# Token tiles and first weights issued from two queues, and the first two projected tiles made in halves

## What is computed

```
h    = rmsnorm(x, norm1_g)                      # x: 512 x 1024
proj = h @ w_in                                 # w_in: 1024 x 3080
fq, fk, fv, f_logit, sq, sk, sv = split(proj)
fox  = forgetting_attention(fq, fk, fv, cumsum(log_sigmoid(f_logit + b_f)))
sb   = stick_breaking_attention(sq, sk, sv)
x    = x + concat(rmsnorm(fox), rmsnorm(sb)) @ w_out
x    = x + moe(rmsnorm(x), ...)                 # 32 experts, top 4
y    = rmsnorm(x)
```

## Time and profile before

| | |
|---|---|
| median of 3 executions | 1460.68 us |
| lowest and highest | 1460.29 and 1463.81 us |
| the profiled execution, its own time | 1463.33 us |
| its span in the trace | 1461.6 us |
| busy share of the span | PE 98%, DVE 90%, ACT 75%, POOL 26% |
| DMA moved | 451.31 MB |

### The profile page before, as it was taken

How to read it: one execution, slowest core, us unless ns; L and a number is a source line. 1 busy time by engine, 2 the same in 40 slices (tenths; PEclk the granted TensorE clock), 3 DMA queues, 4 the chain that set the end, 5 groups by cost and what they waited for, 6 DMA issues and landing times.

```text
span 1461.6 us, 22338 instructions
## 1 busy us (share of the span) xinstructions
PE 1431.5 (98%) x7068; PEld 1164.4 (80%) x7068; DVE 1308.5 (90%) x1520; ACT 1100.6 (75%) x1345; POOL 380.2 (26%) x177
## 2 busy tenths in 40 slices
PE   9999999999999999999999999999999999999995
PEld 7777787787888888888888888888888888888884
DVE  5778765579999999999999999999999999999997
ACT  5668554357888887888888888888888888888884
POOL 3000000050433333333333333333333333333222
PEclk9999999999999999999999999999999999999998
DMA  8021022269999999999999999999999999999953
GB/s 260 14 74 58 29 87 77 107 240 396 410 391 394 397 389 389 385 382 374 373 380 386 367 379 381 374 371 387 377 368 380 377 377 376 378 376 380 365 219 126
DMA packets 98058, 451.31 MB, mean 309 GB/s; under 512 B 11427, under 2 KB 23715, under 8 KB 65250
## 3 DMA queue, kind: packets, MB, share of 16 engines
q1 hardware_dynamic: 90706, 434.16, 77.1%
q0 software_dynamic: 7312, 16.63, 5.0%
HBM read 440.46 MB, written 18.48 MB: 314 GB/s over the span
## 4 chain that ended last, share of the span: by engine, by line
PE 87%; DVE 7%; ACT 3%; DMA 2%; issue 1%; POOL 0%; SPq 0%; ACTq 0%; POOLq 0%; DVEq 0%
PE zpair L2201 47%; PE bank L2201 24%; PE bank L1901 2%; PE bank L1789 2%; PE bank L1791 2%; PE bank L1790 2%; PE bank L2151 1%; PE bank L2159 1%; DVE stage_lo L1212 1%; DVE lbuf L1292 1%; PE zpair L2170 1%; DMA x_scratch<-qk,sidx 1%; DVE pt_lo L1301 1%; DVE lbuf L1288 0%; DVE cols L1309 0%
## 5 line engine op out<-in xcount | busy, mean ns | idle before, releaser
L1212 DVE TENSOR_TENSOR stage_lo<-ring,stage_hi 128x1024 fp32r<-128x1024 f32 x796 | 947.1, 1220 | 41.0 <-ACT stage_hi L788 12.5
L788 ACT CAST stage_hi<-ring 128x1024 fp32r<-128x1024 f32 x796 | 828.0, 1054 | 171.4 <-PE zpair L2201 141.6
L2201 PE MATMUL zpair<-stage_hi,act_hi 128*128 128x512 f32 x1024 | 322.6, 396 | 0.3 <-DVE act_lo L1605 0.3
L668 POOL COPY sidx<-gtab 96x1 int32 (+1 forms) x31 | 230.3, 7428 | 350.3 <-ACT qk L1098 350.3
L2201 PE MATMUL zpair<-stage_hi,act_lo 128*128 128x512 f32 x1024 | 316.6, 390 | 0.0
L2201 PE MATMUL zpair<-stage_lo,act_hi 128*128 128x512 f32 x1024 | 316.2, 390 | 0.3 <-DVE stage_lo L1212 0.2
L2201 PEld LDWEIGHTS zpair<-stage_lo,act_hi 128*128 128x128 f32 x1024 | 192.1, 188 | 42.3 <-DVE stage_lo L1212 1.1
L2201 PEld LDWEIGHTS zpair<-stage_hi,act_lo 128*128 128x128 f32 x1024 | 192.2, 188 | 41.1
L2201 PEld LDWEIGHTS zpair<-stage_hi,act_hi 128*128 128x128 f32 x1024 | 187.4, 188 | 43.8 <-issue 7.9
L2201 PE MATMUL bank<-stage_hi,act_hi 128*128 128x512 f32 x510 | 159.8, 395 | 0.0
L2201 PE MATMUL bank<-stage_lo,act_hi 128*128 128x512 f32 x510 | 157.1, 389 | 0.0
(11 more groups left out here) (301 smaller groups left out, 1424.8 us busy)
## 6 DMA issues: line engine op xcount, KB each, us to landing
ring<-in_w SPq DMA_DIRECT2D x384, 1024.0 KB, 8.1
ring<-in_w_in SPq DMA_DIRECT2D x12, 1024.0 KB, 5.3
ring<-in_w_out SPq DMA_DIRECT2D x4, 1024.0 KB, 4.8
xs_all<-in_x SPq DMA_DIRECT2D x4, 512.0 KB, 5.7
ring<-in_x SPq DMA_DIRECT2D x4, 512.0 KB, 3.7
tn_scratch<-qk SPq DMA_DIRECT2D x4, 512.0 KB, 2.8
x_scratch<-ring SPq DMA_DIRECT2D x4, 512.0 KB, 3.6
ring<-x_scratch SPq DMA_DIRECT2D x4, 512.0 KB, 5.8
```

Source lines behind the costliest of these rows:

```text
L668: nc.gpsimd.tensor_copy(sidx[:], gtab[:, i:i + 1] if isinstance(i, int) else gtab[:, bass.ds(i, 1)]).then_inc(sidx_copied, 1)
L788: nc.scalar.copy(dst, src).then_inc(split_hi, 1)
L1212: nc.vector.tensor_tensor(dst, src, hi_ap.bitcast(F32), ALU.subtract).then_inc(split_lo, 1)
L2201: mm = pe.matmul(bank[b0 + h][:], w[:, k, :], m[:, j % STAGES, h * BANK:(h + 1) * BANK], start=start and w is T_hi and m is stage_hi, stop ...
```

## The change

SP now issues `g1row` first, then `x` tiles 0 and 2, W0 and W2, and from W4 on as before. ACT issues `x` tiles 1 and 3, W1 and W3, ahead of its table load. On ACT and DVE, the casts and rests of the first four halves are followed by the weight pieces 0 and 1, and only then comes token tile 3. On PE, projected tiles 0 and 1 are both made in halves of 256 tokens: tile 0 on the first half of the tokens, then the transposes of token tile 3, tile 1 on the first half, tile 0 and tile 1 on the second. Tile 1 gets bank 1 in place of bank 5. Ten fillers are added on PE before the first projection.

```diff
         def proj_bank(tile):
 
-            return bank[4 + (tile + (tile >= F_AT)) % 2] if tile else bank[0]
+            return bank[4 + (tile + (tile >= F_AT)) % 2] if tile > 1 else bank[tile]
...
         def _(sp):
-            for t in range(TT):
+            sp.dma_start(g1row[0:1, :], norm1_g[0:1, :]).then_inc(g1_in, 16)
+            for t in (0, 2):
                 sp.dma_start(xs[t], x_d[t * P:(t + 1) * P, :]).then_inc(x_in[t], 16)
-                if t == 0:
-                    sp.dma_start(g1row[0:1, :], norm1_g[0:1, :]).then_inc(g1_in, 16)
-
-            for n in range(W_IN_LOADS):
-                kind, r = n // 6, n % 3
-                c0 = (0 if kind else 3 * HW + NH) + r * HW + n // 3 % 2 * 2 * P
+            for n in (0, 2, *range(4, W_IN_LOADS)):
                 if n >= 4:
                     old = n - 4
                     sp.wait_ge(split_lo, 3 * (2 * (old // 3) + 1) + old % 3 + 1)
...
+                sp.dma_start(w_in_slot(n), w_in_columns(n)).then_inc(full[w_slot(n)], 16)
...
+            for t in (1, 3):
+                act.dma_start(xs[t], x_d[t * P:(t + 1) * P, :]).then_inc(x_in[t], 16)
+            for n in (1, 3):
+                act.dma_start(w_in_slot(n), w_in_columns(n)).then_inc(full[w_slot(n)], 16)
             nc.scalar.preload_act_table_set("natural_log_exp_and_others")
...
             h_scale(2)
-            h_cast(0)
-            h_cast(1)
+            for j in range(4):
+                h_cast(j)
+            hi_early(0)
+            hi_early(1)
             h_scale(3)
-            h_cast(2)
-            h_cast(3)
-            hi_early(0)
             for j in range(4, 8):
                 h_cast(j)
...
             h_scaled(2)
-            h_rest(0)
-            h_rest(1)
+            for j in range(4):
+                h_rest(j)
+            lo_early(0)
+            lo_early(1)
             h_scaled(3)
-            h_rest(2)
-            h_rest(3)
-            lo_early(0)
             for j in range(4, 8):
                 h_rest(j)
...
+            for j in range(6):
+                if j in (2, 4):
+                    pe.wait_ge(consts, 4)
+                    keep_busy(4, 4 if j == 2 else 8)
+                turn_h(j)
+            pe.wait_ge(h_lo, 1)
+            keep_busy(0, 10)
             pe.wait_ge(h_lo, 4)
             keep_busy(1, 8)
...
+            def project_half(tile, half):
+
+                pe.wait_ge(split_lo, tile + 1)
+                pe.wait_ge(h_lo, 4 * half + 4)
+                ts = slice(2 * half * P, 2 * (half + 1) * P)
...
-            pe.wait_ge(split_lo, 1)
-            for half in range(2):
-                pe.wait_ge(h_lo, 4 * half + 4)
-                for k in range(KT):
-                    project_half(k, half)
-            for tile in range(1, 3):
-                for k in range(KT):
-                    project(tile, k)
+            project_half(0, 0)
+            turn_h(6)
+            turn_h(7)
+            project_half(1, 0)
+            project_half(0, 1)
+            project_half(1, 1)
+            for k in range(KT):
+                project(2, k)
```

More of the change, by code:

```diff
@@ L399, in turned_at, with w_in_slot, w_in_columns @@
             return obank[m] if s % TT else zpair[s % 2][:, m, :]
+        def w_in_slot(n):
+            return slot(w_slot(n)).rearrange("p (k n) -> p k n", k=KT)
+        def w_in_columns(n):
+            kind, r = n // 6, n % 3
+            c0 = (0 if kind else 3 * HW + NH) + r * HW + n // 3 % 2 * 2 * P
+            return w_in_d.rearrange("(k p) n -> p k n", p=P)[:, :, c0:c0 + 2 * P]
         def moe_slot(c):
@@ L460, in _ @@
                     sp.wait_ge(split_lo, 3 * (2 * (old // 3) + 1) + old % 3 + 1)
-                sp.dma_start(slot(w_slot(n)).rearrange("p (k n) -> p k n", k=KT),
-                             w_in_d.rearrange("(k p) n -> p k n", p=P)[:, :, c0:c0 + 2 * P]).then_inc(full[w_slot(n)], 16)
+                sp.dma_start(w_in_slot(n), w_in_columns(n)).then_inc(full[w_slot(n)], 16)
             for m in range(W_OUT_LOADS):
@@ L941, in scale_of_norm @@
                 nc.scalar.activation(rm[:, cs], rsm[:, cs], ACT.Exp, scale=-0.5).then_inc(rsm_ready, 1)
-            hi_early(1)
             hi_early(2)
@@ L1362, in add_oproj @@
                                                op0=ALU.mult, op1=ALU.add).then_inc(x2_add, 1)
-            for g in range(1, STAGES):
+            for g in range(2, STAGES):
                 lo_early(g)
@@ L1811, in _, with turn_h @@
             pe.wait_ge(consts, 1)
-            for j in range(2 * TT):
+            def turn_h(j):
                 t, h = j // 2, j % 2
-                if j in (2, 4):
-                    pe.wait_ge(consts, 4)
-                    keep_busy(4, 4 if j == 2 else 8)
                 pe.wait_ge(h_norm, t + 1)
@@ L1820, in _ @@
                 mm.then_inc(h_turned, 1)
+            for j in range(6):
[5 more added lines that the diff above has]
+            keep_busy(0, 10)
             pe.wait_ge(h_lo, 4)
             keep_busy(1, 8)
[L1824 to L1829, removed]
+            def project_half(tile, half):
[3 more added lines that the diff above has]
+                for k in range(KT):
+                    ks = slice(k * P, (k + 1) * P)
+                    mm = three(proj_bank(tile)[:, ts], stage_hi[:, tile, ks], stage_lo[:, tile, ks],
+                               hT_hi[:, k, ts], hT_lo[:, k, ts], k == 0, k == KT - 1)
+                if half:
                     mm.then_inc(used, 1)
```

## The result

Over 22 executions each, the changed kernel takes 1463.57 us in the median and the kernel before 1462.14. The ratio is 1.0012, with a 95% interval of 1.0007 to 1.0018: slower by 1.0 to 2.6 us, which is less than the 0.3% that was set as the bound for a change that can be told. The forecast was 1462.3, +1.6 us against the three runs then known, in a range of 1459.4 to 1465.7. The three runs known then had their median at 1460.68, 1.5 us under that of the 22, so the forecast is best compared as a difference: +1.6 us against 1.0 to 2.6.

What follows compares the result with a forecast made beforehand. PE bounds the kernel, mostly in the untouched expert stage; only the first projection's start and its stretch to the first scores could move. +0.5 and +1.1 made +1.6 us, 1462.3 us against the 1460.68 median; range 1459.4 to 1465.7.

Steps and rivals of the forecast that it cites:

- The test: First projection to first attention scores: a shift of the first scores shifts the end one to one.
- Two queues: Loads on SP and ACT: paired loads share bandwidth, W0 lands at 15.6, start moves from 17.40 to 17.9, +0.5 us.
- the sum: Whole kernel: +0.5 us at the start of the projection and +1.1 us for transposes in the stream, +1.6 us.
- Token tile 0: First token load: lands between 4.13 and 6.87, late end taken; the delay is hidden by W0's landing.
- Halves: PE's projection stream: eight transposes of token tile 3 inside it cost +1.1 us; 256-column pieces cost nothing.
- Tile 3 in time: Token tile 3 ready for PE at 20.8, as the first half of tile 0 ends: a tie, nothing taken.
- Later pieces: W2, query's low part, W4: each covered, no cost; thinnest cover 0.3 us, query's low part at 30.2.
- Fillers: Ten more on PE ahead of the first projection, 0.13 us each, put at no cost.
- The early landing: Rival at the start: W0 lands as soon as before, start at 16.3, total 0, 1460.7 us; chance 0.12.
- ACT held: Rival: ACT stuck issuing loads; until 9.5 +3.8 us (chance 0.08), until 12.4 +6.7 us, 1467.4 (chance 0.12).
- the sign of "under 2 us": Sign of a right prediction: ACT's four load issues take under 2 us together.
- The lower clock: Rival: PE idles 1.8 us before the projection, clock falls to 0.50; +3.1 us, 1463.8; chance 0.06.

Runs made afterwards that it cites:

- e11_three_on_act: Changed kernel with W2's load moved to ACT as well, between W1 and W3; ratio to the kernel before 1.0051.
- e6_best: As e5_order, with the gain row's load first on SP and without the ten added fillers; ratio to the kernel before 0.9994.
- e7_x_only: Changed kernel with ACT issuing only token tiles 1 and 3, all weights on SP in order; one execution, 1465.5 us (before: 1463.03).
- e2_halves: Changed kernel with every load back on SP in the old order, halves and ten fillers kept; ratio to the kernel before 1.0009.
- e8_no_turn: As e1_queues, with tile 1 made in halves too and no transposes in the stream; one execution, 1462.1 us (before: 1463.03).
- e5_order: As e2_halves, with token tile 3's roots and casts 4 and 5 moved ahead of weight piece 1's high part; ratio to the kernel before 1.0000.
- e9_no_fillers: Changed kernel without its ten added fillers on PE; ratio to the kernel before 1.0012.
- e1_queues: Kernel before with only the loads split over SP and ACT, gain row first, old order otherwise; ratio to the kernel before 1.0006.

## Why the prediction was right, point by point

- **The test** (when the projection starts, and how long to the first scores) held: the scores moved by 2.24 us and the end by 1.0 to 2.6, and in e11_three_on_act by 7.47 and 7.5. In the other kernels the end differs from the shift of the scores by up to 0.8 us either way, inside the noise of a median; e6_best alone does not fit (scores 0.81 later, ratio 0.9994), and its profile is not a typical one.
- **Two queues, +0.5 forecast, +1.08 measured.** The size was too small, and half of the path was missing. The term was W0's landing, taken as 15.6 from its partner's row; it was 16.1. W1, issued at 1.71 and so before W0 (2.09), landed at 1.7 + 13.3 = 15.0, so the two were 1.1 us apart.
- **What the sum left out is PE's own queue.** It had the casts end at 14.3 and the last filler at 16.1, with PE idle until the start. They ended at 15.66 and 18.48, because between token tile 0's multiply and the first projection PE has 7.6 us of transposes and fillers to do, one behind the other (10.91 to 18.48). So token tile 0 was not hidden behind W0: ACT had 0.42 us to spare, PE none. e7_x_only, where W0 is in time, starts at 18.54 all the same, and e11_three_on_act took 13.1 us for the path that was put at 10.7.
- **Token tile 0** landed at 7.5, beyond my late end of 6.87, and tile 1, its partner, at 4.6. Of this pair it was not the first issued that landed late: tile 0 was issued second.
- **Halves, +1.1 forecast, +1.16 measured**, luck in part, as it is made of other parts: 0.79 for the transposes where I had 1.1, and about 0.4 for tile 1 in halves where I had nothing.
- **Tile 3 in time**: a tie was forecast, and it was there 0.3 us ahead. e2_halves shows the wait that stands behind this tie.
- **Later pieces**: W2 was waited for by ACT (0.3 us at 23.46) and by nobody on PE; the query's low part ended at 29.6 and projected tile 2 began at 30.93.
- **Fillers**: put at nothing; they end within 0.1 us of the low part. Right by luck of a tie.
- **The early landing** did not come with two queues; it is what one queue gives (12.4 or earlier in e2_halves). By the rule of the Trainium skill, page DMA: Bandwidth & Descriptors, section "Issuing engines are not separate DMA queues", two issuers save only the time of the issue. The trace agrees for the loads taken together: the last token tile landed at 9.1 instead of 9.5, the later of W0 and W1 at 16.1 instead of 15.6. Single loads changed places: token tile 1 landed at 4.6 instead of 6.9.
- **ACT held**: ACT's W3 took 2.18 us to issue, so its four issues took 3.6 us together and not 1.7, against the sign of "under 2 us". ACT was ready at 5.7, hidden because token tile 0 was late; at its old landing of 4.1 ACT would have come to it 1.6 us late, and what that costs at the start no run shows. The reading of the earlier trace rows was right that two token tiles and two weight loads just fit, and one more does not. The rule of the Trainium skill, page Perfetto Trace Analysis, section "Per-instruction lifecycle", that the block is locked for one load at a time, is not what held ACT in e11_three_on_act: its last issue stood from 4.25 to 10.6, while SP's only weight load of that time had been issued at 2.10 in 0.45 us. The same four weight loads, two on each queue in the changed kernel, were all issued by 5.12, so it is the backlog of the own queue that holds. Whether there is such a lock besides, these rows cannot say: SP's issue from 2.57 to 5.12 and ACT's from 2.20 to 4.38 overlap, but a row does not tell waiting from writing.
- **The lower clock** did come, in the rows from 7 to 15 us and so ahead of the projection (last section), which is one of the signs of "wrong". It cost little: the transposes of tile 0 took 1.94 us as before, those of tile 1 1.51 instead of 1.36. The idle time in which it was feared, 1.8 us ahead of the projection, did not exist.

Why the two profiled spans are equal: the change's 2.2 us are still there at the routing (PE's matmuls on `pay` start at 319.15 and 321.32), and are lost behind it in this one pair. PE's first transposes of gathered rows stand at 322.41 and 323.54, and those of the second expert at 343.08 and 343.31, before and after:

```profile
319.15 1.23 PE L2100 MATMUL zpair<-pay,ohslot 128*96 128x64 f32 x12
...
322.41 0.85 PE L2151 MATMUL bank<-identF,qk 96*128 96x96 f32 x8 [1.69 <-DMA qk<-tn_scratch,gtab]
...
343.08 0.83 PE L2151 MATMUL bank<-identF,qk 96*128 96x96 f32 x8
```

```profile
321.32 1.23 PE L2116 MATMUL zpair<-pay,ohslot 128*96 128x64 f32 x12
...
323.54 0.85 PE L2167 MATMUL bank<-identF,qk 96*128 96x96 f32 x8 [0.65 <-DMA qk<-tn_scratch,gtab]
...
343.31 0.82 PE L2167 MATMUL bank<-identF,qk 96*128 96x96 f32 x8
```

In the kernel before PE waited 1 us longer for the gathered rows, and then the clock was at 0.50; in the changed one it stayed at 1.00 throughout. That the wait brought the clock down is not shown: e8_no_turn waited 1.38 us at this place and kept 1.00. Stretches of 4 us from 322, before and after (length, busy us by engine, granted clock, DMA share, GB/s):

```profile
322.00:326.00 4.00, 3.59 (x20) 3.11 (x21) 3.81 (x5) 0.95 (x3) 1.84 (x3) 0.66 0.67 214
```

```profile
322.00:326.00 4.00, 3.28 (x29) 2.49 (x27) 4.00 (x4) 0.94 (x3) 2.41 (x4) 1.00 0.50 171
```

This looks like a draw of the execution and not of the kernel. From the first scores to the second expert's transposes it is 306.7 us in the changed kernel and 306.8 in e8_no_turn, the two profiles without a low clock at the routing. The other eleven have one: e5_order takes 307.3, e9_no_fillers, with two, 310.8, and the rest 308.4 to 308.8. The times of all executions fit this. The changed kernel's 22 make two groups, thirteen from 1463.11 to 1463.67 and eight from 1464.38 to 1465.37, with one more at 1467.81; its profiled execution, 1463.30, is of the lower group. The kernel before has eleven up to 1461.91 and eleven from 1462.37 on, with less of a gap; its profiled execution, 1463.33, is of the upper. From lower group to lower group the change costs 2.1 us in the mean, from upper to upper 1.9 (without the one at 1467.81), close to the 2.24 of the first scores. One profile of each kernel would have shown no difference; 22 runs do.

## What to carry to other kernels

A second queue does not make loads faster when the DMA engines are already busy; it changes which load is late. Here the weights that are needed first landed 3 us later for sharing with the next ones, and the token tile that is needed first landed behind the one that the other queue issued ahead of it; either is a loss wherever that load is waited for. Follow every path to the stage that is to start, the engine's own queue of small work too, and not only the one that looks longest. Before DMA issues are put on an engine that computes, look at how long the issues of the present queue are and what stands behind them: here two weight loads were hidden and a third cost another 5.2 us at the first scores. And where a step is moved out of a wait into a full stream, its price is paid nearly in full (0.79 of 1.04 us), so the start has to come earlier by more than the step.

## What the runs showed of the hardware

- An issuing engine is held by its own backlog: 0.46, then 2.03, then 6.35 us for three loads of 1 MB in a row behind two of 512 KB.
- PE's speed in the first 15 us differs between executions. The spreading of the gain took 2.12 us in the changed kernel and 1.98 in e2_halves, and 3.78 in the other eleven. I had put it down as fixed. The granted clock in the rows does not explain it. In the changed kernel it falls to 0.50 (1.2 in place of 2.4 GHz) between 7 and 8 us, PE having done nothing from 6.9 to 10.9; in e2_halves too, in a gap of only 0.7 us. In e11_three_on_act it stays at 1.00 over a gap of 6 us. Yet the transposes of tile 0 took 1.94 us in all three. In this part of the span the duration of a known instruction says more than that column; why, stays open.

```profile
8.00:10.00 2.00, 0.00 (x0) 0.00 (x0) 0.64 (x1) 1.94 (x5) 1.21 (x2) 0.50 1.07 376
10.00:12.00 2.00, 1.09 (x5) 1.12 (x6) 1.89 (x4) 1.90 (x7) 2.00 (x5) 0.50 1.10 350
```

- At the routing, near 310 to 326 us, profiles of nearly the same instructions had the low clock for very different lengths: not at all in two, and in e1_queues from before 314 to after 322 (the rows below). It is worth some 1.9 us in most of them, as much as the whole change, though not in proportion to its length: 3.4 us of it cost 0.6 in e5_order and 2.0 in the kernel before. What decides it was not tried.

```profile
314.00:318.00 4.00, 4.00 (x33) 3.34 (x31) 1.90 (x6) 3.99 (x5) 0.14 (x1) 0.50 0.99 371
318.00:322.00 4.00, 4.00 (x21) 2.51 (x22) 3.73 (x13) 0.22 (x1) 2.83 (x5) 0.50 0.57 195
```
